# A hybrid decoder layer on one NeuronCore: the router's turned rows move to two one-tile buffers, two down weights are loaded earlier, and a mask moves by one unit

## The chip, the cores and the metric

The kernel runs on one core of one Trainium2 chip (trn2). The metric is the device time of one execution in microseconds (us). The profile is that of one execution, and times in it are us from the start of its span.

## The reference, cut to what matters

One layer (DEPTH is 1) on 512 tokens of width 1024, all in float32. Three residual blocks, then a final RMS norm:

```python
x = x + hybrid_mixer(rmsnorm(x, mix_norm_g), ...)       # 8 heads of forgetting attention | HGRN2 | convolution
x = x + cross_attention(rmsnorm(x, xatt_norm_g), mem_n, w_xq, w_xkv, w_xo)
x = x + hierarchical_moe(rmsnorm(x, ffn_norm_g), ...)   # 4 groups, top 1; 4 experts in a group, top 2
return rmsnorm(x, final_norm_g)
```

Forgetting attention adds to each score the difference of two cumulated log decays and masks it causally, then takes a softmax. In the mixture of experts a router picks one group and two of its four experts for each token; an expert is silu(h Wg) * (h Wu) times Wd, with Wg and Wu 1024 x 256 and Wd 256 x 1024, so 3 MB of weights for each of the 16 experts.

## The kernel before, in words

Each engine runs one list of instructions in order, and semaphores tie the lists together. The parts that the change touches are three.

**The attention over 16 units (lines 2104 to 2173 on TensorE, 1531 to 1597 on VectorE, 960 to 1006 on ScalarE).** A unit is one pair of heads and one block of 128 queries; four units make a pair of heads, and unit `u` has `u % 4 + 1` blocks of keys. In round `u` TensorE multiplies queries by keys (`qk(u)`, L2111), multiplies probabilities of unit `u - 3` by values (`pv`, L2133), turns the probabilities of unit `u - 2` (`pt`, L2120), and in some rounds does one product for the memory (L1904 or L1914) that fills the time. VectorE in round `u` adds the decay to the scores and takes the extremum (`f_scores(u)`, L1542), copies half of the turned probabilities (`f_pt(u - 2)`, L1560; ScalarE copies the other half, L973) and divides by the sums (`f_scale(u)`, L1553). The decays of a pair of heads come from `lf_dram` with four DMAs on the SP queue (`decay_sums`, L517). There are two buffers for them, so SP issues those of pair `p` (2 or 3) when the scores of pair `p - 2` are done. `f_mask(p)` (L1578, two instructions) adds the causal mask to the decays of pair `p`; it waits for their DMAs, and VectorE does it in round `4 (p - 1) + 1`, ahead of `f_pt`. The first scores of pair `p`, in round `4 p`, wait for it.

**The router.** After the cross attention TensorE multiplies by `w_xo` (L2180). In between, for each tile `t` of 128 tokens, it turns the rows of the residual (`turn_half`, L1674) into two PSUM banks. VectorE multiplies each bank by the norm's gain and writes it to `hT` (`turn_evac`, L1063, for stage 3), in the columns of tile `t`, so all four tiles have room of their own. TensorE multiplies `hT` by the router's weights (`logits_half`, L1680). The region `A[:, 7680:8704]` holds the final norm's gain (`fgain`), which SP loads at L535 behind two down weights; VectorE waits for it (`router_in`) before its last adds (L1333).

**The experts.** Rows of tokens are gathered into 12 passes (0 to 11) of 128 rows, and each pass serves two experts. TensorE does in pass `p`: gate and up (`gate_up_pass`, L1780, 64 matmuls), turning the next pass's rows (L1762), down of the pass before (`down_pass(p - 1)`, L1806, 32 matmuls), and turning the hidden rows (L1767). POOL gathers the rows of a pass (L648) and stores its result (L640). After the last passes it gathers each token's two results (L665), when the stores have landed.

The weights come on the SP queue in the order in which the passes take up experts (`TAKEN` is 0, 3, 1, 2, 4, 7, 5, 6, 8, 11, 9, 10, 12, 15, 13, 14). Gate and up have five homes (four slots of `W`, and `n_sb`); down weights have six, four in `Dn` and two in `hT` (`DN_HOME[e] >= SLOTS`, experts 4 and 7 first). SP's list (`experts_loads`, L519 to 584) is: down weights of 3 and 2; when the queries' projections are done (`freed(12)`, `freed(13)`), gate and up of 0 and 3; when cross attention is done (`xo_ps`), down weights of 0 and 1, and `fgain`; the normed rows to DRAM (L539); gate and up of 1, 2 and 4; then a wait for the last logits and for the rows of the second pass (`xg_in[1]`), and the down weights of 4 and 7 into `hT`; then, pass by pass, a wait for the pass that frees a home (`gu_ps`, `y_ps`) and the next loads (L476, L480, L488), 32 loads of 1 MB.

Expert weights first used in pass 9 are those of 12 and 15, in pass 10 those of 13, in pass 11 those of 14.

Of the kernel before, what the change touches and what calls it, by code (L numbers as in the profile page):

```python
# [10 lines left out]
ALU = mybir.AluOpType  # L11
# [3 lines left out]
P = 128  # L15
# [4 lines left out]
D = 1024  # L20
# [10 lines left out]
NG, NE = 4, 4  # L31
EX = NG * NE
# [3 lines left out]
DC = D // P  # L36
# [71 lines left out]
def build(nc, x, mem, mix_norm_g, w_in, fox_f_bias, fox_norm_g, hgrn_lb_logits, hgrn_norm_g,  # L108
# [3 lines left out]
    with ExitStack() as ctx:  # L112
# [87 lines left out]
        hidT = A[:, 5120:5632].rearrange("p (b k t) -> p b k t", b=2, k=2)  # L200
        ysb = A[:, 5632:7680].rearrange("p (b d) -> p b d", b=2)
        fgain = A[:, 7680:8704]

        room = [8704]

# [223 lines left out]
        def pair_end(u):  # L429

            return (u - PV_LAG) // ST if u >= PV_LAG and (u - PV_LAG) % ST == ST - 1 else None
# [50 lines left out]
        def load_gate_up(sp, e):  # L482
            load_gate(sp, e)
            load_up(sp, e)

        def load_down(sp, e):
            h = DN_HOME[e]
            sp.dma_start(dn_at[h], wd_e[e]).then_inc(dn_loaded[h], 16)  # L488
# [30 lines left out]
        def experts_loads(sp):  # L519

            sp.wait_ge(router_step, 6)
            sp.dma_start(y_dram[ZERO_ROW:ZERO_ROW + 1, :].rearrange("o (p n) -> (o p) n", p=P), zero8).then_inc(n_stored, 16)
            sp.wait_ge(x1_done, 8)
            for e in TAKEN[:DN_HOMES]:
                if DN_HOME[e] in (1, 3):
                    load_down(sp, e)
            for k in range(2):
                sp.wait_ge(*freed(12 + k))
                load_gate_up(sp, TAKEN[k])

            sp.wait_ge(xo_ps, 2 * XH)
            for e in TAKEN[:DN_HOMES]:
                if DN_HOME[e] in (0, 2):
                    load_down(sp, e)
            sp.dma_start(fgain, final_norm_g.rearrange("(o d) -> o d", o=1).to_broadcast([P, D])).then_inc(router_in, 16)  # L535

            def store_rows(t):
                sp.wait_ge(n_done, NORM0[3] + t + 1)
                sp.dma_start(n_dram[t * P:(t + 1) * P, :], nA[:, t, :]).then_inc(n_stored, 16)  # L539

            for t in range(ST - 1):
                store_rows(t)

            sp.wait_ge(*freed(14))
            load_gate(sp, TAKEN[2])
            store_rows(ST - 1)
            load_up(sp, TAKEN[2])
            load_gate_up(sp, TAKEN[3])
            load_gate_up(sp, TAKEN[4])
            sp.wait_ge(logits_ps, ST)  # L550
            sp.wait_ge(xg_in[1], 16)
            for e in TAKEN[:DN_HOMES]:
                if DN_HOME[e] >= SLOTS:
                    load_down(sp, e)

            for p in range(NP):
                if GU_REFILL[p]:
                    sp.wait_ge(gu_ps, p + 1)
                    for e in GU_REFILL[p]:
                        load_gate_up(sp, e)  # L560
                if p >= 1 and DN_REFILL[p - 1]:
                    sp.wait_ge(y_ps, 2 * p)
                    for e in DN_REFILL[p - 1]:
                        load_down(sp, e)

            sp.wait_ge(over_done, 1)
            with sp.If(sp.value_load(over[0:1, 0:1]) > 0):
                sp.wait_ge(y_ps, 2 * NP)
                with sp.Fori(0, OVER_PARTS * EX) as k:

                    e = k % EX
                    sp.dma_start(W[:, 0, :, 0:FF], wg_e[e]).then_inc(ov_w, 16)
                    sp.dma_start(W[:, 0, :, FF:2 * FF], wu_e[e]).then_inc(ov_w, 16)
                    sp.dma_start(Dn[:, 0], wd_e[e]).then_inc(ov_w, 16)
                    sp.wait_ge(ov_y_sb, 2 * k + 2)
                    sp.dma_start(ov_rows[k], ov_y).then_inc(ov_stored, 16)
            with sp.Else():
                pass
            for t in range(ST):
                sp.wait_ge(fin_out, t + 1)  # L580
                if t == ST - 1:
                    sp.wait_ge(fin_sq, ST + 1)
                sp.dma_start(out[0, t * P:(t + 1) * P, :], x_out[:, t, :]).then_inc(out_done, 16)
            sp.wait_ge(out_done, 16 * ST)
# [475 lines left out]
        def turn_evac(dve, stage, t, k, bank, dst, r0):  # L1060

            dve.wait_ge(turned, TURN0[stage] + 2 * t + k + 1)
            nc.vector.tensor_tensor(dst[:, 4 * k:4 * k + 4, t * P:(t + 1) * P], bank[:, :].rearrange("p (c t) -> p c t", c=4),  # L1063
                                    pc[:, r0 + 4 * k:r0 + 4 * k + 4].rearrange("p (c o) -> p c o", o=1).to_broadcast([P, 4, P]),
                                    ALU.mult).then_inc(turn_sb, 1)
# [5 lines left out]
        def experts_dve(dve):  # L1071
# [29 lines left out]
            def full_mean(t):  # L1101
                n = NORM0[3] + t
                dve.wait_ge(sq_done, NORM0[3] + 2 * t + 2)
                nc.vector.tensor_scalar(ss[:, n:n + 1], ss[:, n:n + 1], half_ss[:, t:t + 1], 1.0 / D, ALU.add, ALU.mult).then_inc(ms_done, 1)

            def choose(t):

                n = NORM0[3] + t
                dve.wait_ge(logits_ps, t + 1)
                dve.wait_ge(rstd_done, n + 1)  # L1110
                link(nc.vector.scalar_tensor_tensor(out=logits[:, t], in0=PS[6][:, t * (NG + EX):(t + 1) * (NG + EX)],
                                                    scalar=rstd[:, n:n + 1], in1=rbias, op0=ALU.mult, op1=ALU.add))
                sets = logits[:, t].rearrange("p (s k) -> p s k", k=4)
                steps[0] += 1
                nc.vector.tensor_tensor(above, across_rows(sets), across_cols(sets), ALU.is_ge).then_inc(route, 1)
                link(nc.vector.tensor_tensor(beats, across_rows(sets), across_cols(sets), ALU.is_gt))
                low = lower.rearrange("p (o i) j -> p o i j", o=1).to_broadcast([P, 1 + NG, 4, 4])
                link(nc.vector.copy_predicated(beats, low, above))
                link(nc.vector.tensor_reduce(rank, beats, AX_X, ALU.add))
                link(nc.vector.tensor_tensor(chosen[:, t], rank, limit, ALU.is_lt))  # L1120
                nc.vector.tensor_tensor(pickedb[:, t].rearrange("p (g e) -> p g e", g=NG), chosen[:, t, 1:],
                                        ghot[:, t].rearrange("p (g o) -> p g o", o=1).to_broadcast([P, NG, NE]), ALU.mult).then_inc(picked_done, 1)
                nc.vector.tensor_tensor(tokg16[:, t], ghot[:, t], tokid[:, t:t + 1].to_broadcast([P, NG]), ALU.mult).then_inc(pick_done, 1)
# [11 lines left out]
                    nc.vector.tensor_scalar(first_pick[:, t, r], pick[:, t, j, 0:r.stop - r.start], rstd[:, n:n + 1], ghot[:, t, 0:1],  # L1135
                                            ALU.mult, ALU.mult).then_inc(pick_done, 1)

            gains = pc[:, R_FFN:R_FFN + DC]

            def turned_rows(p):  # L1140

                if p >= 2:
# [10 lines left out]

            for t in range(ST):
                if t:
                    turn_evac(dve, 3, t - 1, 1, PS[5], hT, R_FFN)
                    full_mean(t - 1)
                    if t == 1:
                        dve.wait_ge(router_in, 16 * 4)
                        dve.wait_ge(router_const, 8)  # L1160
                    choose(t - 1)
                add_half(t, 0)
                turn_evac(dve, 3, t, 0, PS[4], hT, R_FFN)
                if t:
                    place(t - 1)
                first_mean(t)
                add_half(t, 1)
            turn_evac(dve, 3, ST - 1, 1, PS[5], hT, R_FFN)
            full_mean(ST - 1)
            choose(ST - 1)  # L1170
            place(ST - 1)
# [194 lines left out]
        def _(dve):  # L1366
# [215 lines left out]
            for u in range(UNITS + PV_LAG):  # L1582
                if u < UNITS:
                    for a in range(2):
                        f_scores(u, a)
                if pair_end(u) is not None:
                    f_out(pair_end(u))
                if u % ST == 1 and u < UNITS - ST:
                    f_mask(u // ST + 1)
                if TURN_LAG <= u < UNITS + TURN_LAG:  # L1590
                    f_pt(u - TURN_LAG)
                if u < UNITS:
                    for a in range(2):
                        f_scale(u, a)
                if u and pair_end(u - 1) is not None:
                    f_norm(pair_end(u - 1))
            f_norm(FH // 2 - 1)
# [68 lines left out]
        def experts_pe(pe, project_some):  # L1666
# [10 lines left out]
            def logits_half(t, k):  # L1677
                pe.wait_ge(turn_sb, TURN0[3] + 2 * t + k + 1)
                for c in range(4 * k, 4 * k + 4):
                    mm = nc.tensor.matmul(PS[6][:, t * (NG + EX):(t + 1) * (NG + EX)], hT[:, c, t * P:(t + 1) * P], wgr[:, c, :],  # L1680
                                          start=c == 0, stop=c == DC - 1)
                if k:
                    mm.then_inc(logits_ps, 1)
# [602 lines left out]
```

## Time and profile before

| what | value |
|---|---|
| median of 3 runs | 720.63 us (720.16 to 722.01) |
| the profiled execution's own time | 721.87 us |
| its span, first to last instruction | 720.1 us |
| PE busy | 683.2 us (95%) |
| DVE, ACT, POOL busy | 281.8, 152.1, 76.8 us |
| DMA | 111.91 MB, mean 155 GB/s |
| mean granted TensorE clock | 0.992 |
| chain that ended last | PE 80%, DMA 7%, SPq 4%, DVE 3%, ACT 3% |

The span has 1.8 us less than the execution's own time. PE is TensorE's matmuls, PEld its weight loads, DVE VectorE, ACT ScalarE, POOL GpSimd, SP the sync engine, SPq and POOLq their DMA issues. A line number is that of the helper which issues the instruction. "Idle before" is the time in which an engine did nothing ahead of an instruction, with what ended it; "issue" stands where no releaser was found in the records. The DMA share is the mean busy share of the core's 16 DMA engines, whose transfers overlap a little, so full use shows as somewhat over 1.

### The profile page before, as it was taken

How to read it: one execution, taken by the hardware profiler on the slowest of the kernel's cores; microseconds unless marked ns; L12 is line 12 of the kernel's file. 1: busy time of each engine (PE TensorE's matmuls, PEld its weight loads, DVE VectorE, ACT ScalarE, POOL GpSimd, SP SyncE). 2: the span in 40 equal slices, each digit the busy share in tenths (PEclk: the TensorE clock that was granted, in tenths of full speed). 3: DMA queues.
4: the chain of work that ended last, by engine and by line, in shares of the span. 5: the costliest groups of instructions: out<-in, count | busy, mean ns of one | idle time of the engine just before them, and what ended most of it. 6: DMA issues, size and time to landing. Idle time of an engine off the chain costs nothing.

```text
span 720.1 us, 8431 instructions
## 1 busy us (share of the span) xinstructions
PE 683.2 (95%) x3398; PEld 333.3 (46%) x3398; DVE 281.8 (39%) x673; ACT 152.1 (21%) x313; POOL 76.8 (11%) x106
## 2 busy tenths in 40 slices
PE   6999999999989899999999999999999999998993
PEld 4744444453547565444444446545564333332331
DVE  3207599927144564303120006413335712212156
ACT  3010351003282444211000003302111110101012
POOL 2000081502020000000000000000001110100052
PEclk9999999999999999999999999999999999999997
DMA  8903240303035513300019403030139999999773
GB/s 255 333 0 117 76 158 1 118 2 117 24 124 151 176 60 117 117 1 0 1 32 395 157 0 117 2 144 29 51 96 351 380 374 383 383 377 382 263 230 121
DMA packets 69941, 111.91 MB, mean 155 GB/s; under 512 B 5649, under 2 KB 43781, under 8 KB 69901
## 3 DMA queue, kind: packets, MB, share of 16 engines
q1 hardware_dynamic: 65724, 96.16, 38.8%
q0 software_dynamic: 4176, 15.21, 5.7%
q8 instruction: 27, 0.44, 0.3%
q14 instruction: 14, 0.11, 0.0%
HBM read 101.90 MB, written 9.46 MB: 155 GB/s over the span
## 4 chain that ended last, share of the span: by engine, by line
PE 80%; DMA 7%; SPq 4%; DVE 3%; ACT 3%; issue 1%; POOL 1%; DVEq 0%; POOLq 0%; ACTq 0%
PE bank L1904 26%; PE bank L2180 15%; PE bank L1780 8%; PE bank L1914 6%; PE bank L1806 3%; DMA W<-in_w_up_dram 2%; PE bank L2250 2%; PE bank L1950 2%; PE bank L2230 2%; DMA n_sb<-y_dram,A 2%; PE bank L1936 2%; PE bank L2133 1%; DMA x_sb<-in_x_dram 1%; SPq L480 1%; PE bank L2111 1%
## 5 line engine op out<-in xcount | busy, mean ns | idle before, releaser
L1904 PE MATMUL bank<-hT,W 128*128 128x512 f32 x368 | 159.7, 593 | 0.9 <-DVE hT L1063 0.9
L2180 PE MATMUL bank<-W,n_sb 128*128 128x512 f32 x256 | 114.2, 596 | 0.7 <-ACT n_sb L1031 0.7
L1904 PEld LDWEIGHTS bank<-hT,W 128*128 128x128 f32 x368 | 69.4, 190 | 87.5 <-issue 86.0
L1780 PE MATMUL bank<-W,A 128*32 128x512 f32 x672 | 84.8, 594 | 5.5 <-issue 2.4
L2180 PEld LDWEIGHTS bank<-W,n_sb 128*128 128x128 f32 x256 | 47.1, 190 | 53.9 <-issue 52.3
L1413 DVE SCALAR_TENSOR_TENSOR A<-A,pc 128x511 f32<-128x511 f32 (+29 forms) x60 | 51.6, 860 | 2.0
L1780 PEld LDWEIGHTS bank<-W,A 128*32 128x32 f32 x672 | 23.9, 110 | 52.9 <-issue 50.9
L695 POOL TENSOR_TENSOR rstd<-ss,mhalf 128x1 f32<-128x1 f32 x14 | 7.7, 549 | 372.8 <-DVE ss L1047 208.3
L1806 PE MATMUL bank<-Dn,A 128*32 128x512 f32 x264 | 36.3, 595 | 0.0
L1262 DVE TENSOR_TENSOR A<-A,bank 128x256 f32<-128x256 f32 x12 | 5.1, 421 | 75.8 <-ACT A L825 75.8
L898 ACT ACTIVATE A<-bank 128x512 f32<-128x512 f32 (+1 forms) x22 | 12.1, 556 | 103.7 <-PE bank L1904 77.0
L1904 PE MATMUL bank<-Dn,W 128*128 128x256 f32 x128 | 30.9, 397 | 1.2 <-DVE Dn L1063 1.0
L1621 DVE TENSOR_REDUCE fmx<-bank 128x1 f32<-128x256 f32 x16 | 6.7, 421 | 62.4 <-PE bank L2230 62.3
L1780 PE MATMUL bank<-n_sb,A 128*32 128x512 f32 x96 | 28.2, 594 | 0.0
L1914 PE MATMUL bank<-W,Dn 128*128 128x512 f32 x64 | 28.2, 594 | 0.0
L1904 PEld LDWEIGHTS bank<-Dn,W 128*128 128x128 f32 x128 | 24.9, 199 | 5.3 <-issue 1.2
L1806 PE MATMUL bank<-hT,A 128*32 128x512 f32 x120 | 25.4, 595 | 0.5 <-ACT A L832 0.5
L1478 DVE SCALAR_TENSOR_TENSOR states<-states,Dn,bank 128x64 f32<-128x64 f32 x64 | 17.9, 280 | 18.9 <-issue 13.9
L1063 DVE TENSOR_TENSOR hT<-bank,pc 128x512 f32<-128x512 f32 x24 | 16.0, 686 | 19.8 <-PE bank L1674 10.8
L825 ACT ACTIVATE A<-bank 128x256 f32<-128x256 f32 x12 | 4.6, 384 | 84.8 <-PE bank L1780 84.8
L964 ACT ACTIVATE hT<-hT,fmx 128x128 f32<-128x128 f32 (+3 forms) x32 | 17.7, 554 | 20.7 <-DVE fmx L1542 20.7
L1914 PE MATMUL bank<-W,hT 128*128 128x512 f32 x48 | 21.2, 594 | 0.0
(306 smaller groups left out, 806.8 us busy)
## 6 DMA issues: line engine op xcount, KB each, us to landing
W<-in_w_gate_dram SPq DMA_DIRECT2D x14, 1024.0 KB, 14.5
W<-in_w_up_dram SPq DMA_DIRECT2D x14, 1024.0 KB, 15.1
Dn<-in_w_down_dram SPq DMA_DIRECT2D x11, 1024.0 KB, 13.6
W<-in_w_in_dram SPq DMA_DIRECT2D x5, 2048.0 KB, 9.2
W<-in_w_xkv_dram SPq DMA_DIRECT2D x4, 2048.0 KB, 8.2
hT<-in_w_down_dram SPq DMA_DIRECT2D x5, 1024.0 KB, 12.9
y_dram<-A POOLq DMA_DIRECT2D x10, 512.0 KB, 7.0
W<-in_w_out_dram SPq DMA_DIRECT2D x2, 2048.0 KB, 7.8
```

The costliest lines, as they stand in the source:

```text
L964: nc.scalar.activation(fs[u % 3][a][:, 0:w], fs[u % 3][a][:, 0:w], ACT.Exp, bias=fmx[:, k:k + 1], scale=-1.0, accum_out=frs[:, k:k + 1]).t ...
L1063: nc.vector.tensor_tensor(dst[:, 4 * k:4 * k + 4, t * P:(t + 1) * P], bank[:, :].rearrange("p (c t) -> p c t", c=4), pc[:, r0 + 4 * k:r0 + ...
L1413: nc.vector.scalar_tensor_tensor(out=y[:, s:S], in0=a[:, 0:S - s], scalar=pc[:, r:r + 1], in1=y[:, s:S], op0=ALU.mult, op1=ALU.add).then_i ...
L1478: nc.vector.scalar_tensor_tensor(out=states[:, k + 1, :], in0=states[:, k, :], scalar=he4[:, p, k * CHUNK + CHUNK - 1:k * CHUNK + CHUNK], ...
L1780: mm = nc.tensor.matmul(PS[2 + b][r, :], xgT[:, b, c, r], gu_at[GU_HOME[e]][:, c, :], start=c == 0, stop=c == DC - 1)
L1806: mm = nc.tensor.matmul(PS[5 + n][r, :], hidT[:, p % 2, k, r], dn_at[DN_HOME[e]][:, k, 512 * n:512 * n + 512], start=k == 0, stop=k == 1)
L1904: mm = nc.tensor.matmul(bank[0:w, 0:n], lhs, src[:, c, 0:n], start=c == 0, stop=c == DC - 1)
L1914: mm = nc.tensor.matmul(bank[:, 0:w], src[:, c, t * P:(t + 1) * P], W[:, slot, c, col:col + w], start=c == 0, stop=c == DC - 1)
L1936: mm = nc.tensor.matmul(bank[:, 0:IW], hT[:, c, t * P:(t + 1) * P], w_if[:, c, :], start=c == 0, stop=c == DC - 1)
L1950: mm = nc.tensor.matmul(bank[:, :], lhs, hT[:, c, :], start=c == 0, stop=c == DC - 1)
L2180: mm = nc.tensor.matmul(PS[k % 4][:, :], src[:, c, t * P:(t + 1) * P], W[:, (n_load + n) % SLOTS, c, :], start=first and j == 0, stop=last ...
L2230: mm = nc.tensor.matmul(PS[u % 2][:, 0:M], xqT[:, 2 * h + k, t * P:(t + 1) * P], xkT[:, 2 * h + k, :], start=k == 0, stop=k == 1)
```

## The change

The router's turned rows go to `routeT`, two buffers of one tile, at `A[:, 4096:5120]` and `A[:, 7680:8704]`; tile `t` uses buffer `t % 2`, and `hT` isn't used by the router any more. The down weights of experts 4 and 7 are loaded right behind gate and up of expert 3, with no wait of their own, and the wait for the second pass's rows is gone. `fgain` shares its region with the second buffer, so its load moves behind all weights. `f_mask(p)` moves from round `4 (p - 1) + 1`, ahead of `f_pt`, to round `4 (p - 1) + 2`, behind `f_scale`.

```diff
--- before.py
+++ after.py
@@ -200,6 +200,7 @@
         hidT = A[:, 5120:5632].rearrange("p (b k t) -> p b k t", b=2, k=2)
         ysb = A[:, 5632:7680].rearrange("p (b d) -> p b d", b=2)
         fgain = A[:, 7680:8704]
+        routeT = [A[:, 4096:5120].rearrange("p (c t) -> p c t", c=DC), A[:, 7680:8704].rearrange("p (c t) -> p c t", c=DC)]
 
         room = [8704]
 
@@ -527,12 +528,14 @@
             for k in range(2):
                 sp.wait_ge(*freed(12 + k))
                 load_gate_up(sp, TAKEN[k])
+            for e in TAKEN[:DN_HOMES]:
+                if DN_HOME[e] >= SLOTS:
+                    load_down(sp, e)
 
             sp.wait_ge(xo_ps, 2 * XH)
             for e in TAKEN[:DN_HOMES]:
                 if DN_HOME[e] in (0, 2):
                     load_down(sp, e)
-            sp.dma_start(fgain, final_norm_g.rearrange("(o d) -> o d", o=1).to_broadcast([P, D])).then_inc(router_in, 16)
 
             def store_rows(t):
                 sp.wait_ge(n_done, NORM0[3] + t + 1)
@@ -547,11 +550,6 @@
             load_up(sp, TAKEN[2])
             load_gate_up(sp, TAKEN[3])
             load_gate_up(sp, TAKEN[4])
-            sp.wait_ge(logits_ps, ST)
-            sp.wait_ge(xg_in[1], 16)
-            for e in TAKEN[:DN_HOMES]:
-                if DN_HOME[e] >= SLOTS:
-                    load_down(sp, e)
 
             for p in range(NP):
                 if GU_REFILL[p]:
@@ -563,6 +561,8 @@
                     for e in DN_REFILL[p - 1]:
                         load_down(sp, e)
 
+            sp.wait_ge(logits_ps, ST)
+            sp.dma_start(fgain, final_norm_g.rearrange("(o d) -> o d", o=1).to_broadcast([P, D])).then_inc(router_in, 16)
             sp.wait_ge(over_done, 1)
             with sp.If(sp.value_load(over[0:1, 0:1]) > 0):
                 sp.wait_ge(y_ps, 2 * NP)
@@ -1103,6 +1103,15 @@
                 dve.wait_ge(sq_done, NORM0[3] + 2 * t + 2)
                 nc.vector.tensor_scalar(ss[:, n:n + 1], ss[:, n:n + 1], half_ss[:, t:t + 1], 1.0 / D, ALU.add, ALU.mult).then_inc(ms_done, 1)
 
+            gains = pc[:, R_FFN:R_FFN + DC]
+
+            def route_evac(t, k):
+
+                dve.wait_ge(turned, TURN0[3] + 2 * t + k + 1)
+                nc.vector.tensor_tensor(routeT[t % 2][:, 4 * k:4 * k + 4, :], PS[4 + k][:, :].rearrange("p (c t) -> p c t", c=4),
+                                        gains[:, 4 * k:4 * k + 4].rearrange("p (c o) -> p c o", o=1).to_broadcast([P, 4, P]),
+                                        ALU.mult).then_inc(turn_sb, 1)
+
             def choose(t):
 
                 n = NORM0[3] + t
@@ -1135,8 +1144,6 @@
                     nc.vector.tensor_scalar(first_pick[:, t, r], pick[:, t, j, 0:r.stop - r.start], rstd[:, n:n + 1], ghot[:, t, 0:1],
                                             ALU.mult, ALU.mult).then_inc(pick_done, 1)
 
-            gains = pc[:, R_FFN:R_FFN + DC]
-
             def turned_rows(p):
 
                 if p >= 2:
@@ -1153,19 +1160,19 @@
 
             for t in range(ST):
                 if t:
-                    turn_evac(dve, 3, t - 1, 1, PS[5], hT, R_FFN)
+                    route_evac(t - 1, 1)
                     full_mean(t - 1)
                     if t == 1:
                         dve.wait_ge(router_in, 16 * 4)
                         dve.wait_ge(router_const, 8)
                     choose(t - 1)
                 add_half(t, 0)
-                turn_evac(dve, 3, t, 0, PS[4], hT, R_FFN)
+                route_evac(t, 0)
                 if t:
                     place(t - 1)
                 first_mean(t)
                 add_half(t, 1)
-            turn_evac(dve, 3, ST - 1, 1, PS[5], hT, R_FFN)
+            route_evac(ST - 1, 1)
             full_mean(ST - 1)
             choose(ST - 1)
             place(ST - 1)
@@ -1585,13 +1592,13 @@
                         f_scores(u, a)
                 if pair_end(u) is not None:
                     f_out(pair_end(u))
-                if u % ST == 1 and u < UNITS - ST:
-                    f_mask(u // ST + 1)
                 if TURN_LAG <= u < UNITS + TURN_LAG:
                     f_pt(u - TURN_LAG)
                 if u < UNITS:
                     for a in range(2):
                         f_scale(u, a)
+                if u % ST == 2 and u < UNITS - ST:
+                    f_mask(u // ST + 1)
                 if u and pair_end(u - 1) is not None:
                     f_norm(pair_end(u - 1))
             f_norm(FH // 2 - 1)
@@ -1677,7 +1684,7 @@
             def logits_half(t, k):
                 pe.wait_ge(turn_sb, TURN0[3] + 2 * t + k + 1)
                 for c in range(4 * k, 4 * k + 4):
-                    mm = nc.tensor.matmul(PS[6][:, t * (NG + EX):(t + 1) * (NG + EX)], hT[:, c, t * P:(t + 1) * P], wgr[:, c, :],
+                    mm = nc.tensor.matmul(PS[6][:, t * (NG + EX):(t + 1) * (NG + EX)], routeT[t % 2][:, c, :], wgr[:, c, :],
                                           start=c == 0, stop=c == DC - 1)
                 if k:
                     mm.then_inc(logits_ps, 1)
```

## Rows read from the trace of the kernel before

**Rows 1.** Busy by stage: us; PE, PEld, DVE, ACT, POOL; PEclk; DMA share, GB/s.
```profile
440.00:466.00 26.00, 25.06 (x98) 15.78 (x96) 15.44 (x52) 10.33 (x29) 0.00 (x0) 1.00 0.00 1
...
544.00:653.00 109.00, 105.35 (x930) 35.65 (x930) 37.34 (x111) 13.42 (x29) 13.95 (x18) 1.00 1.07 377
```

**Rows 2.** PE, order of time, passes 2, 9, 10: start, us, what [idle before].
```profile
565.67 7.07 PE L1780 MATMUL bank<-W,A 128*32 128x512 f32 x64
...
653.24 7.07 PE L1780 MATMUL bank<-W,A 128*32 128x512 f32 x64 [1.53 <-DMA W<-in_w_up_dram]
...
667.71 7.07 PE L1780 MATMUL bank<-W,A 128*32 128x512 f32 x64 [2.44 <-issue]
```

**Rows 3.** SP, order of time: start, us the issue took, what.
```profile
551.06 4.12 SPq L488 DMA_DIRECT2D hT<-in_w_down_dram  x2
...
555.23 1.19 SPq L476 DMA_DIRECT2D W<-in_w_gate_dram  x1
...
574.91 0.62 SPq L476 DMA_DIRECT2D W<-in_w_gate_dram  x1
...
637.13 6.05 SPq L480 DMA_DIRECT2D W<-in_w_up_dram  x1
...
648.76 8.03 SPq L480 DMA_DIRECT2D W<-in_w_up_dram  x1
...
666.94 3.88 SPq L488 DMA_DIRECT2D hT<-in_w_down_dram  x1
```

**Rows 4.** DMA issues, us to landing last: those of 555.23, 637.13, 648.76, 666.94.
```profile
W<-in_w_gate_dram SPq DMA_DIRECT2D x1, 1024.0 KB, 15.6
...
W<-in_w_up_dram SPq DMA_DIRECT2D x1, 1024.0 KB, 16.0
...
W<-in_w_up_dram SPq DMA_DIRECT2D x1, 1024.0 KB, 18.9
...
hT<-in_w_down_dram SPq DMA_DIRECT2D x1, 1024.0 KB, 12.7
```

**Rows 5.** Chain that ended last, 238 to 249: start, us, what.
```profile
238.66 7.92 DMA A<-lf_dram
...
247.89 0.61 DVE hT L1560
```

**Rows 6.** PE, order of time, the stall in round 6.
```profile
248.63 1.10 PE L2133 MATMUL bank<-hT,A 128*64 128x128 f32 x16 [1.95 <-DVE hT L1560]
```

**Rows 7.** VectorE, order of time: a mask, and the scores of rounds 3, 7, 11.
```profile
229.34 1.29 DVE L1578 TENSOR_TENSOR Dn<-Dn,causal 128x256 f32<-128x256 f32 x2 [2.05 <-DMA Dn<-lf_dram]
...
235.89 0.69 DVE L1542 CUSTOM_DVE_ANT_0 hT<-bank,A 128x512 f32<-128x512 f32 x1 [1.87 <-PE bank L2111]
...
254.66 0.69 DVE L1542 CUSTOM_DVE_ANT_0 hT<-bank,Dn 128x512 f32<-128x512 f32 x1 [2.45 <-PE bank L2111]
...
271.63 0.69 DVE L1542 CUSTOM_DVE_ANT_0 hT<-bank,A 128x512 f32<-128x512 f32 x1 [2.44 <-PE bank L2111]
```

**Rows 8.** Groups of 466 to 680: a dense and a spread target.
```profile
L1147 DVE TENSOR_TENSOR A<-bank,pc 128x512 f32<-128x512 f32 x24 | 15.5, 682 | 1.1 <-PE bank L1719 1.0
...
L1063 DVE TENSOR_TENSOR hT<-bank,pc 128x512 f32<-128x512 f32 x8 | 5.5, 692 | 10.8 <-PE bank L1674 10.8
```

**Rows 9.** The page, part 5: weight loads from two layouts.
```profile
L1904 PEld LDWEIGHTS bank<-hT,W 128*128 128x128 f32 x368 | 69.4, 190 | 87.5 <-issue 86.0
...
L1904 PEld LDWEIGHTS bank<-Dn,W 128*128 128x128 f32 x128 | 24.9, 199 | 5.3 <-issue 1.2
```

**Rows 10.** DMA issues, us to landing last: those of 466.97 and 467.44.
```profile
Dn<-in_w_down_dram SPq DMA_DIRECT2D x1, 1024.0 KB, 7.0
...
A<-in_final_norm_g_dram SPq DMA_DIRECT2D x1, 512.0 KB, 7.8
```

**Rows 11.** Chain that ended last, where the passes end.
```profile
680.69 3.21 DMA y_dram<-A
```

**Rows 12.** The page, part 6: POOL's stores.
```profile
y_dram<-A POOLq DMA_DIRECT2D x10, 512.0 KB, 7.0
```


## The prediction

> **What bounds the kernel now.** I read the table of busy time by stage first: it shows which resource is full in which stretch. In the twelve expert passes up to 653 PE is busy 105.4 of 109 us, and the DMA engines are full too, at 1.07 and 377 GB/s [rows 1]. Of two full resources the one that ends a wait is the bound, so PE's order of time is next: two passes start late, pass 9 by 1.53 us, for an up weight, and pass 10 by 2.44 us, where no releaser was found [rows 2]. The issues with their landings name that one. Expert 15's up weight, issued at 637.13, landed 16.0 later at 653.1, just ahead of pass 9's start at 653.24; expert 13's, issued at 648.76, landed 18.9 later at 667.7, and pass 10 starts at 667.71 [rows 2 to 4]. So TensorE sets the pace of the passes, but the weights run so close behind that TensorE loses 1.53 + 2.44 = 3.97 us to them.
>
> Did weights come late because SP issued them late, or because the engines were full? In SP's order of time the issues themselves last several us (8.03, 6.05, 4.12) and follow each other: SP pushes into a full queue [rows 3]. Expert 7's gate (issued 555.23) landed at 570.8, expert 14's down at 679.6, with 31 loads of 1 MiB between: 3.51 us each [rows 3, 4].
>
> The third reading is the chain of waits through the attention. It runs over the decays' transfer (issued 238.66, 7.92 us), the mask and VectorE's copy `f_pt(3)`, which stands behind the mask and was done at 248.5 [rows 5]; PE then stood 1.95 us [rows 6]. Its 1.95 us are the only stall that the mask's place makes.
>
> **Part 1: two down weights earlier.** Removed from the full stretch are two loads (experts 4 and 7, 2.10 MB) and the wait ahead of them. How far does everything behind them come forward? With POOL's traffic unchanged the engines need 2 x 3.51 = 7.0 us less. The lower bound is bytes alone, 2.10 MB at 377 GB/s, 5.6 us [rows 1]. I take 7.0, since POOL's gathers and stores are tied to the passes and don't grow, and keep 5.6 as the other end. Needed for no stall: expert 15's up weight 1.5 us earlier, and expert 13's 3.97 earlier, since pass 10 then starts 1.53 + 2.44 earlier. Even 5.6 covers that, with 1.6 us to spare. So 3.97 come off, from 0 to 3.97 in the range.
>
> Next in line is the release of homes. SP can't issue expert 5's gate before pass 1's gate and up end, or expert 6's before pass 2's, at 565.67 + 7.07 = 572.7; before, it did so at 574.91, only 2.2 us later [rows 2, 3]. After the change SP does wait there. It costs nothing if the engines still have work: a load lands some 15 us after its issue [rows 4], and with 7.0 taken off about 7 us of transfers are still queued at 572.7. From there on SP again pushes into a full queue.
>
> The two loads go out right behind gate and up of expert 3, near 433, and move past nothing that is pressed for time: SP's next wait ends with the cross attention at 466, and from 440 to 466 the engines carry 1 GB/s [rows 1]. Their 2.10 MB take 5.6 us of these 26. Cost 0; without this cover they would cost what they cost now. Their target `hT` is free, as the queries' last product is what SP waits for there. The wait for the second pass's rows (`xg_in[1]`) goes as well: the issues at 551.06 [rows 3] stood behind it, and its time is within the 7.0.
>
> **Part 2: the router's buffers.** VectorE has the same eight evacuations, now with a dense target. The nearest rows are 692 ns for the spread target `hT` and 682 for a dense one [rows 8]: -0.08 us for eight, nothing. TensorE's 64 weight loads read another layout; by the rows of two layouts (190 and 199 ns [rows 9]) that is 64 x 9 ns = 0.6 us either way at most, and they run beside matmuls. I take 0 and keep -0.6 to +0.6. No wait is added: VectorE writes a buffer a second time only after TensorE has turned the tile two later, which on its list stands behind the products that read the buffer.
>
> **Part 3: the final gain.** Its load leaves 467 and goes to the end of SP's list. At 467.44 it landed 7.8 us after its issue, at 475.2, and the down weight before it (466.97 + 7.0) at 474.0, so its own part is 1.2 us; these are the bounds [rows 10]. The wait for the last logits that is put before it is long met. Expert 14's down lands at 679.6 - 7.0 = 672.6, and with 1.2 the gain is there at 673.8. Whom can it delay? POOL's last store, which ends the chain of the passes (issued 680.69, landed 3.21 later [rows 11]) and would be issued at 680.69 - 3.97 = 676.7, 2.9 us behind it. Cost 0, up to 3.7 if it took all of its 7.8 from 672.6 (to 680.4). VectorE needs it only in its last adds, after the gathers that follow this store.
>
> **Part 4: the mask one unit later.** The same six instructions, 1.29 us a pair [rows 7]. In round 1 the mask waited 2.05 us for its transfer, but PE lost nothing. In round 5 the copy no longer stands behind it: it can follow `pt(3)` at once, and `pv(3)` follows TensorE's `qk(6)`: 1.95 us come off. In its new place the mask stands between `f_scale` of round 2, 6 or 10 and the scores of the next round, before which VectorE is idle 1.87, 2.45 and 2.44 us [rows 7]. The mask of 1.29 fits in each. Its transfer is there at 246.6 (238.66 + 7.92 [rows 5]). Round 6 reaches the mask at about 250: VectorE was free 2.45 us ahead of 254.66, at 252.2, and all that is 1.95 earlier. If one didn't fit, it would cost up to 1.29, three of them 3.9. I take 0.
>
> **Sum.** 3.97 + 1.95 = 5.92 us. The profiled execution took 721.87, so its like would take 715.95; it stood 1.24 above the median of 720.63, so I forecast 714.7. The two savings add, because all behind 250 shifts together: the loads' waits there are for TensorE's own progress.
>
> **The rivals.**
> *A, both savings* (the forecast): 714.7. For it: 1.6 us to spare at pass 10 even by the lower bound, and 1.87 - 1.29 = 0.6 at the tightest mask.
> *B, the mask finds a new victim.* The scores of round 7 come late, or ScalarE's half of the copy becomes what `pv` waits for, and the 1.95 stay. Against it: 2.45 idle us for 1.29. 720.63 - 3.97 = 716.7.
> *C, the queue follows its releases.* If the loads come forward only by as much as expert 6's gate can be issued earlier (2.2 us) and not by the bytes saved, expert 13's up weight lands at 665.5, and of 3.97 only 2.2 come off: 720.63 - 1.95 - 2.2 = 716.5. Against it: about 7 us of transfers are queued at that time.
> *D, hidden anyway.* TensorE's late starts have another cause than the weights, and it merely moves on from the attention's stall to another: 719 to 720.6. Pass 10's missing releaser speaks for it, the landings to 0.1 us against it.
> *E, slower: the gain at the tail.* SP's list keeps its pace, the last weight still lands at 679.6, and behind it come the gain's 0.5 MB. At the upper bound it lands at 687.4, and if POOL's last store, issued at 680.7, has to stand behind it, all gathers start 6.7 us later: 720.63 - 1.95 + 6.7 = 725.4. It decides from a landing after 680.7 + 1.95 + 2.2 = 684.9. Against it: its own part was 1.2 us, and POOL's stores landed 7.0 us after issue, in the middle [rows 12], beside weights that took 13 to 19 [rows 4].
> The Trainium skill's "DMA: Bandwidth & Descriptors" (section "Queues, rings and completion order") bears on E: each DMA engine goes round the queues that have work for it, so a store of POOL's shares with SP's queue and doesn't stand behind it. By that rule, the trace agrees, as its stores landed twice as fast as SP's loads, and E shrinks to the time of the gain's own 0.5 MB. The same page (section "Anatomy of one DMA") gives an estimate for a lone transfer of 2.0 us and the bytes at 436 GB/s, 3.2 us for the gain, where the trace has 1.2 behind another; by 3.2 it lands at 675.8, still ahead of the store.
>
> **How the numbers follow.** What a measurement can tell from no change is 0.3%, 2.2 us, so faster means under 718.5. A 0.60, B 0.12, C 0.16: all faster, 0.88. D 0.08: the same. E 0.04: slower. The range has to hold 8 in 10: A, with 0.6 for the router's loads and the runs' own spread below (714.7 - 1.3 = 713.4), and B and C above, with the same 0.6, to 717.3. D and E are left out.
>
> **What would show it.** In the changed profile: passes 9 and 10 start 12.0 us after the one before, with no idle time for a weight; the up weights of 15 and 13 land 5 us and more ahead of them; the last down weight lands about 7 us earlier against pass 11, and the gain before POOL's last store. SP shows a real wait before expert 6's gate. The round-6 stall of 1.95 is gone, VectorE's masks stand in its idle time, and no scores of rounds 3, 7 and 11 start behind one. The passes' DMA share stays at 1.07 but ends earlier. It is wrong if PE's idle time before pass 9 or 10 stays (C or D), if `pv` in round 6 still waits (B), or if the last store takes much over 3.2 us (E).

## The result, and the profile after

In five runs of each, the changed kernel took a median of 713.46 us (712.26 to 714.91) against 720.63 (717.93 to 722.01) before: a ratio of 0.9896, 95% interval 0.9872 to 0.992. Faster by 7.5 us by the ratio (9.2 to 5.8 by its interval), where 5.9 were forecast; 0.9896 x 720.63 = 713.1 lies 0.3 below the low end of the range.

| profiled execution | before | after |
|---|---|---|
| time, span, us | 721.87, 720.1 | 714.91, 713.2 |
| PE on the chain that ended last | 80% | 87% |
| DMA and SPq on that chain | 7% and 4% | 4% and 0% |
| mean granted clock | 0.992 | 0.991 |

Line numbers behind 1150 are 7 higher in the changed kernel (L1780 is L1787, L1904 is L1911), SP's loads 1 higher. Three lines of the page after: the span, the engines' busy time, and the chain by engine.

```profile
span 713.2 us, 8430 instructions
...
PE 682.8 (96%) x3398; PEld 332.3 (47%) x3398; DVE 282.0 (40%) x673; ACT 152.0 (21%) x313; POOL 76.0 (11%) x106
...
PE 87%; DMA 4%; DVE 3%; ACT 3%; issue 1%; POOL 1%; SPq 0%; DVEq 0%; POOLq 0%; ACTq 0%
```

PE holds 87% of the chain, and SP's queue is off it. The next view is busy time by stage, beside [rows 1] (columns as there).

```profile
440.00:466.00 26.00, 24.37 (x91) 14.69 (x90) 12.87 (x44) 9.86 (x27) 0.00 (x0) 1.00 0.10 34
544.00:650.00 106.00, 104.11 (x926) 35.37 (x922) 34.99 (x99) 12.11 (x27) 12.67 (x17) 1.00 1.07 377
```

The two down weights, issued from 430.05 on, are mostly in by 440 and all near 442: only their last 0.7 MB fall between 440 and 466, where there was nothing (34 GB/s for 1). The passes run at the same 1.07 and 377 GB/s. PE in order of time (start, us, what, idle before and its releaser) tells what that brought:

```profile
215.43 5.38 PE L1911 MATMUL bank<-Dn,W 128*128 128x256 f32 x16 [0.99 <-DVE Dn L1063]
...
246.04 1.09 PE L2140 MATMUL bank<-hT,A 128*64 128x128 f32 x16
...
247.34 3.62 PE L1911 MATMUL bank<-Dn,W 128*128 128x256 f32 x16
...
563.00 7.07 PE L1787 MATMUL bank<-W,A 128*32 128x512 f32 x64
...
588.57 0.63 PE L1823 MATMUL bank<-identf,states 128*128 128x128 f32 x4 [1.14 <-DVE A L1262]
...
648.96 7.07 PE L1787 MATMUL bank<-W,A 128*32 128x512 f32 x64
...
660.92 7.07 PE L1787 MATMUL bank<-W,A 128*32 128x512 f32 x64
```

Passes 9 and 10 start 12.0 us after the pass before, with no idle time: the 1.53 and 2.44 of [rows 2] are gone. So is the 1.95 of [rows 6]: the products at 246.04 follow without a gap. Left in the passes are 0.78 and 0.76 ahead of the first two, and the 1.14 at 588.57. The row at 215.43 is for later: 16 products that take 5.38 us here and 3.62 to 3.72 elsewhere in the attention. The kernel before has the like of it:

```profile
216.11 5.38 PE L1904 MATMUL bank<-Dn,W 128*128 128x256 f32 x16 [0.98 <-DVE Dn L1063]
```

This also dates the difference. The two traces are 0.68 us apart here, by chance in the first loads; after the mask's stall 2.7, behind passes 9 and 10 6.8, and at the end 6.9. So the profiled pair gained 0.7 (chance) + 2.0 + 4.1 + 0.1.

SP's order of time (start, us the issue took), then four of its landings (us from issue to landing, last: those of 626.64, 638.65, 656.48 and 662.54), then the store of the chain's end:

```profile
430.05 2.60 SPq L489 DMA_DIRECT2D hT<-in_w_down_dram  x2
...
562.76 2.64 SPq L489 DMA_DIRECT2D Dn<-in_w_down_dram  x1
...
570.13 0.37 SPq L477 DMA_DIRECT2D W<-in_w_gate_dram  x1
...
626.64 6.57 SPq L481 DMA_DIRECT2D W<-in_w_up_dram  x1
...
638.65 7.42 SPq L481 DMA_DIRECT2D W<-in_w_up_dram  x1
...
656.48 6.02 SPq L489 DMA_DIRECT2D hT<-in_w_down_dram  x1
...
662.54 0.71 SPq L565 DMA_DIRECT2D A<-in_final_norm_g_dram  x1
```

```profile
W<-in_w_up_dram SPq DMA_DIRECT2D x1, 1024.0 KB, 18.1
...
W<-in_w_up_dram SPq DMA_DIRECT2D x1, 1024.0 KB, 21.0
...
hT<-in_w_down_dram SPq DMA_DIRECT2D x1, 1024.0 KB, 15.3
...
A<-in_final_norm_g_dram SPq DMA_DIRECT2D x1, 512.0 KB, 10.4
```

```profile
673.91 3.20 DMA y_dram<-A
```

The early pair is issued at 430.05. SP comes to expert 6's gate at 565.4 and then really waits, until pass 2's gate and up end at 563.00 + 7.07 = 570.07. Expert 15's up weight lands at 644.7, 4.2 us ahead of pass 9, expert 13's at 659.6, 1.3 ahead of pass 10. Expert 14's down lands at 671.8, the gain at 672.9, and POOL's last store, issued at 673.91, takes 3.20, as before [rows 11]. Last, VectorE's masks in their new place:

```profile
232.79 1.29 DVE L1585 TENSOR_TENSOR Dn<-Dn,causal 128x256 f32<-128x256 f32 x2
...
235.21 0.69 DVE L1549 CUSTOM_DVE_ANT_0 hT<-bank,A 128x512 f32<-128x512 f32 x1 [1.12 <-PE bank L2118]
...
249.53 1.28 DVE L1585 TENSOR_TENSOR A<-A,causal 128x256 f32<-128x256 f32 x2
...
252.06 0.69 DVE L1549 CUSTOM_DVE_ANT_0 hT<-bank,Dn 128x512 f32<-128x512 f32 x1 [1.25 <-PE bank L2118]
...
268.96 0.69 DVE L1549 CUSTOM_DVE_ANT_0 hT<-bank,A 128x512 f32<-128x512 f32 x1 [1.24 <-PE bank L2118]
```

Each mask follows other work at once, and the scores behind it still wait for PE (1.12, 1.25 and, in round 11, 1.24 us): it fits.

### The profile page after: what moved, and what is told of

Read it like the earlier page. It is cut to its first block, busy times and chain, and to the rows that moved or that the text cites. A ratio compares the mean times of both kernels' runs of the same rounds, so it can differ in the third digit from the quotient of the medians.

```text
span 713.2 us, 8430 instructions
## 1 busy us (share of the span) xinstructions
PE 682.8 (96%) x3398; PEld 332.3 (47%) x3398; DVE 282.0 (40%) x673; ACT 152.0 (21%) x313; POOL 76.0 (11%) x106
## 4 chain that ended last, share of the span: by engine, by line
PE 87%; DMA 4%; DVE 3%; ACT 3%; issue 1%; POOL 1%; SPq 0%; DVEq 0%; POOLq 0%; ACTq 0%
PE bank L1911 26%; PE bank L2187 16%; PE bank L1787 11%; PE bank L1921 6%; PE bank L1813 5%; PE bank L2257 2%; PE bank L1957 2%; PE bank L2237 2%; PE bank L2140 2%; DMA n_sb<-y_dram,A 2%; PE bank L1943 2%; PE bank L1769 1%; PE bank L2118 1%; DMA x_sb<-in_x_dram 1%; PE bank L2127 1%; PE bank L2029 1%
## 5 line engine op out<-in xcount | busy, mean ns | idle before, releaser
L1911 PE MATMUL bank<-hT,W 128*128 128x512 f32 x368 | 159.7, 593 | 0.9 <-DVE hT L1063 0.9
L1911 PEld LDWEIGHTS bank<-hT,W 128*128 128x128 f32 x368 | 69.4, 190 | 87.5 <-issue 86.0
L1787 PE MATMUL bank<-W,A 128*32 128x512 f32 x672 | 84.8, 594 | 1.5 <-DVE A L1154 1.5
L1787 PEld LDWEIGHTS bank<-W,A 128*32 128x32 f32 x672 | 23.2, 110 | 49.5 <-issue 47.6
L1911 PE MATMUL bank<-Dn,W 128*128 128x256 f32 x128 | 30.9, 397 | 1.2 <-DVE Dn L1063 1.0
L1787 PE MATMUL bank<-n_sb,A 128*32 128x512 f32 x96 | 28.2, 594 | 0.0
L1911 PEld LDWEIGHTS bank<-Dn,W 128*128 128x128 f32 x128 | 24.9, 199 | 5.3 <-issue 1.2
L1095 DVE TENSOR_TENSOR x_sb<-x_sb,bank 128x512 f32<-128x512 f32 x8 | 5.5, 688 | 33.6 <-PE bank L2187 33.6
```

Of the source, the lines that this page charges most:

```text
L1787: mm = nc.tensor.matmul(PS[2 + b][r, :], xgT[:, b, c, r], gu_at[GU_HOME[e]][:, c, :], start=c == 0, stop=c == DC - 1)
L1911: mm = nc.tensor.matmul(bank[0:w, 0:n], lhs, src[:, c, 0:n], start=c == 0, stop=c == DC - 1)
```

## The experiments

Theory: the two savings add, and nothing else happens. Where runs came out above its sum, the rival was that each wait had a price beyond its length. All ratios are to the kernel before, run in the same session; its medians were 722.00, 722.13 and 721.71.

### Each part alone

**The mask alone:** the kernel before with the diff's last hunk but one, `f_mask` at `u % ST == 2` behind `f_scale`.

> The kernel before with the mask alone moved. Theory (two independent savings): the 1.95 us stall in round 6 is gone, the passes keep about 4.0 us of late starts, and the time is 2.0 us under before (ratio 0.997). Rival (the attention's saving is larger than read, because a later stall goes with it): 3 us or more under before, with PE's idle sum between 220 and 310 lower by more than 2.1.

**The loads alone:** the change, with `f_mask` left in its old place.

> The change without the mask's move. Theory: round 6 keeps its 1.95 us, passes 9 and 10 have no stall, 4.0 to 4.2 us under before (ratio 0.994). Rival (the last part of the surprise, 7.2 for 5.9, comes from the loads, in runs whose stalls in the passes are larger than the profiled one's): 5 us or more under before.

**The buffers alone:** `routeT`, `route_evac` and the gain at the end of SP's list; down weights and mask as before.

> The two router buffers and the gain's load at the end; the two down weights back in their old place with both waits, the mask in its old place. Theory: nothing moves, within 0.6 us of before, and passes 9 and 10 start late by 4.0 us together. Rival (the buffers themselves give the missing us, by their dense layout): 1 us under before, with shorter rows in the router.

**The change once more.**

> The changed kernel once more. Theory: the surprise is the runs' spread: 5.9 to 6.3 us under before of the same session (ratio 0.9915), and PE's first stretch up to 30 us varies by some 0.7 us from profile to profile. Rival (a real further saving): 7 us again (ratio 0.990).

| kernel | median us | ratio (95%) |
|---|---|---|
| mask alone | 718.95 | 0.9969 (0.9953 to 0.9985) |
| loads alone | 715.06 | 0.9917 (0.9896 to 0.9939) |
| buffers alone | 721.95 | 1.0004 (0.9987 to 1.002) |
| change again | 713.57 | 0.9889 (0.9865 to 0.9913) |

By the ratios the mask gives 2.2 us (forecast 1.95), the buffers nothing, the loads 6.0 where 3.97 were forecast: most of the excess sits with the loads. PE's order of time in the mask's kernel, then in the buffers' (lines 9 higher than before), shows where:

```profile
664.69 8.77 PE L1780 MATMUL bank<-W,A 128*32 128x512 f32 x64 [2.66 <-issue]
```

```profile
651.40 7.07 PE L1789 MATMUL bank<-W,A 128*32 128x512 f32 x64 [0.83 <-DMA W<-in_w_up_dram]
...
666.16 8.62 PE L1789 MATMUL bank<-W,A 128*32 128x512 f32 x64 [2.72 <-issue]
```

Pass 10's 64 products took 8.77 and 8.62 us in these profiles, 7.07 in [rows 2]. The buffers' kernel by stretches (columns of [rows 1]) says why:

```profile
640.00:651.00 11.00, 10.57 (x98) 3.42 (x86) 2.31 (x4) 1.36 (x3) 1.10 (x2) 1.00 1.06 381
664.00:667.00 3.00, 0.84 (x5) 0.24 (x9) 0.00 (x0) 0.00 (x0) 0.56 (x1) 0.82 1.04 381
667.00:675.00 8.00, 8.00 (x67) 2.42 (x60) 0.00 (x0) 0.15 (x1) 0.00 (x0) 0.85 1.08 380
675.00:680.00 5.00, 5.00 (x46) 1.87 (x48) 2.17 (x4) 1.04 (x3) 0.00 (x0) 1.00 0.43 167
```

The granted clock fell about when the wait ended and came back inside the pass: at the lower of its two levels (1.2 of 2.4 GHz), 0.82 of 3 us and 0.85 of 8 us make 1.1 + 2.4 = 3.5 us, and half of that is lost where PE has work. DMA stays at 381 and 380 GB/s, so the weights aren't what slows the products. The Trainium skill has this in "TensorE: Matmul & The Clock Gate" (section "HAM oscillation — how this bites in real kernels"): a wait for DMA between groups of matmuls lets the array be throttled again, and the next group starts at the lower clock. The trace agrees, with 8.62 - 7.07 = 1.55 us behind a wait of 2.72, though the waits in the page's own example are longer, 3 to 5 us. The profile of before that the prediction rests on happened to keep its clock there.

The router's own rows, in the buffers' kernel:

```profile
L1113 DVE TENSOR_TENSOR A<-bank,pc 128x512 f32<-128x512 f32 x8 | 5.5, 692 | 10.8 <-PE bank L1683 10.8
```

692 ns for the evacuation, as in [rows 8].

### Is it the wait that costs the clock?

**Filled:** the kernel before, with four products that nothing reads in pass 10, ahead of the wait for its weights.

```diff
                 pe.wait_ge(xt_sb, 2 * p + 2)
+                if p == 10:
+                    keep_busy(4, PS[0])
```

> The kernel before, with four more matmuls of scanmask by identf into bank 0 (their product is not used) ahead of pass 10, in the time in which TensorE waits for expert 13's weights; nothing is loaded earlier. Theory (the wait before pass 10 costs its own 2.4 to 2.7 us and, in part of the executions, 1.6 more, since the granted clock then falls to half for a stretch): no half clock around pass 10, the matmuls of the pass in 7.07 and not 8.6 to 8.8 us, and 0.5 to 1.2 us under before (ratio 0.9985), though TensorE does 2 us more work. Rival (the fall is not tied to the wait): the same time as before or up to 0.5 us more, and half clock in pass 10 in some profiles.

**Three more profiles of it, and three of the kernel before.**

> The kernel before with pass 10's wait filled. Theory (the wait brings the fall of the clock): pass 10's 64 matmuls take 7.07 us in this look and in the next two. Rival (the fall goes with the late weights): 8.4 to 8.8 us in most of the three.

> As in the look before it: 7.07 us for pass 10's gate and up if the wait is the cause, 8.4 to 8.8 if not.

> As in the look before it: 7.07 us for pass 10's gate and up if the wait is the cause, 8.4 to 8.8 if not.

> The kernel before, looked at once more, for how often the granted clock falls at pass 10. Theory: passes 9 and 10 wait 3.5 to 4.5 us together in each look, and in more than half of the looks pass 10's gate and up take 8.6 to 8.8 us at half clock for a part. Rival (e1 and e3 were chance): 7.07 in all looks.

> As the look before it: more than half of these looks with half clock in pass 10, or none.

> As the look before it: more than half of these looks with half clock in pass 10, or none.

Filled took 721.91, ratio 0.9988 (0.997 to 1.0006): no change that can be told, 0.9 us by the means. So the times don't decide here, the profiles do. The filler (each product leaves two records) costs 0.7: from pass 9 to pass 10 it is 15.40 us in its four profiles, 14.70 on the mean of six with the bare wait. PE in its second profile, then in the first further profile of the kernel before:

```profile
663.74 3.60 PE L1664 MATMUL bank<-scanmask,identf 128*128 128x512 f32 x8
...
667.27 7.07 PE L1780 MATMUL bank<-W,A 128*32 128x512 f32 x64
```

```profile
246.67 1.09 PE L2133 MATMUL bank<-hT,A 128*64 128x128 f32 x16 [2.35 <-DVE hT L1560]
...
248.17 5.08 PE L1904 MATMUL bank<-Dn,W 128*128 128x256 f32 x16
...
667.25 8.77 PE L1780 MATMUL bank<-W,A 128*32 128x512 f32 x64 [2.87 <-issue]
```

The pass behind the filler took 7.07 in four profiles of four. Behind the bare wait it took 8.77, 8.43 and 8.77 in the three further profiles (waits of 2.87, 2.58 and 2.73). With the two above and the first profile, the clock fell in 5 of 6 profiles with that wait, in none of 4 with it filled. The same data, the same weights, the same place: the idle time is the cause. The further profiles show it a second time: at 248.17, behind the mask's stall, the 16 products took 5.08 for 3.62. By stretches:

```profile
243.00:246.00 3.00, 1.32 (x9) 0.54 (x7) 1.37 (x3) 0.73 (x3) 0.00 (x0) 1.00 0.03 9
246.00:249.00 3.00, 2.33 (x20) 2.04 (x21) 2.93 (x11) 1.05 (x3) 0.00 (x0) 0.79 0.00 0
249.00:252.00 3.00, 3.00 (x10) 2.45 (x9) 1.18 (x5) 0.94 (x4) 0.00 (x0) 0.65 0.00 0
252.00:255.00 3.00, 3.00 (x18) 1.65 (x17) 0.64 (x3) 0.39 (x1) 0.00 (x0) 1.00 0.00 0
```

Ten profiles have the mask's stall (before, loads alone, buffers alone, the three further ones of before, filled's four), and in five of them the clock fell behind it: the three further ones, and two of filled. Of the six without stall or filler (the change three times, mask alone, and one early and late turn below) none has a fall there. The other fall of the attention, near 215, comes ahead of the stall and stands in 3 of those ten and 2 of these six: it has nothing to do with the change. No profile has both: the five falls behind the stall are all among the seven of those ten that had none near 215.

### Do the loads follow the bytes?

**One early:** the change, with only expert 4's down early; expert 7's goes behind gate and up of expert 4 (`TAKEN[4]`; the expectation calls it expert 2), with no wait.

```diff
             for e in TAKEN[:DN_HOMES]:
-                if DN_HOME[e] >= SLOTS:
+                if DN_HOME[e] == SLOTS:
                     load_down(sp, e)
...
             load_gate_up(sp, TAKEN[4])
+            for e in TAKEN[:DN_HOMES]:
+                if DN_HOME[e] == SLOTS + 1:
+                    load_down(sp, e)
```

> The change, but only expert 4's down weight is loaded early; expert 7's goes out behind gate and up of expert 2, with no wait. Theory (bytes): one load is worth 2.7 us, half of the 5.4 that two brought, so pass 9 starts with no wait, pass 10 waits 4.0 - 2.7 = 1.3 us, the clock mostly holds, and the time is 1.3 us above the changed kernel. Rival (the queue follows its releases, so the removed wait was what mattered): no wait at either pass, and the changed kernel's time.

714.68, ratio 0.9898 (0.9873 to 0.9923). PE in this kernel (lines 10 higher than before):

```profile
660.25 7.07 PE L1790 MATMUL bank<-W,A 128*32 128x512 f32 x64 [1.30 <-issue]
```

Pass 9 doesn't wait, pass 10 waits 1.30: the margin of 1.3 that the change had there has become a wait of 1.3, so one load is worth 2.6 us, against 1.05 MB at 377 GB/s = 2.8 and a spacing of 3.51. If the queue followed its releases, taking one load back in would have changed nothing. And after 1.30 the pass still takes 7.07: this wait did not cost the clock. The 1.3 us above the changed kernel that were expected don't show in the times: 0.9898 beside the change's 0.9889 and 0.9896 is 0.1 to 0.7 us, and the intervals cover each other.

### What was left

**Late turn:** the change, with the late tiles turned in passes 2 and 4 instead of 2 and 3 (`if p in (2, 4): turn_late(p // 2 - 1)` on TensorE's list, `if p in (3, 5): late_turned((p - 3) // 2)` on VectorE's).

> The change, with the second turning of the late rows behind pass 4 instead of pass 3. Theory: the 1.14 us in which TensorE waits for VectorE's copy ahead of pass 4 are gone, nothing takes their place as the weights have 1.4 us to spare at pass 10: but then pass 10 starts 1.1 us earlier too, and 0.3 us are left; 1.1 us under the changed kernel, 0.8 if the weights bind again.

**Kept busy:** the change, with two unread products ahead of each of two waits of the attention's start.

```diff
             g = run([along(1, 3, 0, FW)], g, 5)
+            keep_busy(2, PS[2])
...
             pe.wait_ge(ho_rs, HP)
+            keep_busy(2, PS[2])
             pe.wait_ge(turn_sb, TURN0[2])
```

> The change, with two more matmuls into bank 2 (product not used) at each of TensorE's two idle times near 213 and 215. Theory: the half clock that follows there in part of the executions (5.38 for 3.69 us in the 16 matmuls behind it) is gone, the two kinds of runs become one, and the median falls by 0.5 to 1.5 us. Rival (the fall has another cause): half clock stays in the profile, or the time is as the changed kernel's.

**Both:**

> The change with both of the last two edits, the later turning of the late rows and the matmuls that keep TensorE busy near 213 and 215. Theory (they add up): 1.1 us and, in the median, about 0.8 us more under before than the changed kernel, so a ratio of 0.986 to 0.987, and in the profile no half clock before the last gathers and no wait at pass 10. Rival (with both, the weights bind at pass 10 again): a wait of up to 1 us there, ratio 0.988.

| kernel | median us | ratio (95%) |
|---|---|---|
| late turn | 713.06 | 0.9875 (0.9848 to 0.9901) |
| kept busy | 713.12 | 0.9878 (0.9853 to 0.9903) |
| both | 711.91 | 0.9872 (0.9842 to 0.9902) |

Late turn loses the 1.14 of 588.57. In its profile pass 10 starts 12.18 us behind pass 9 (657.52 and 645.34) where it was 11.96, so some 0.2 of it come back there; in that of both it is 11.97. Kept busy, at the two waits:

```profile
214.50 1.88 PE L1671 MATMUL bank<-scanmask,identf 128*128 128x512 f32 x4
...
216.21 3.62 PE L1911 MATMUL bank<-Dn,W 128*128 128x256 f32 x16
```

3.62 for the 16 products that took 5.38 and 5.17 in two of the six profiles with neither stall nor filler, 3.69 in the others. The fillers cost 0.6 us: from the products at 204.94 to those at 215.43 it was 10.49 in the change, here, from 205.04 to 216.21, 11.17, and one gap behind is 0.07 shorter. Both together is the fastest median of all, but its interval and those of the two alone cover each other. A last profile of the change had 712.39 us, no wait at passes 9 and 10, and 3.69 at its row of 215:

> The changed kernel once more: pass 9 and 10 without a wait and at full clock; near 216 the clock may fall or not (it did in one of two profiles), never near 248, where the mask's wait is gone.

### The ledger

Each timed run comes with its mean granted clock. (1 - clock) x time is what the lower level would cost if TensorE had work all the while; before it was 6.3 to 7.1 us a run, in the means of three sessions. Not all of that is lost. In all 18 profiles the clock goes to the lower level behind TensorE's last product and stays there to the end. The change again, by stretches:

```profile
705.00:712.40 7.40, 0.00 (x0) 0.00 (x0) 2.19 (x4) 0.72 (x1) 1.36 (x2) 0.61 0.54 214
```

PE is idle there, so these 0.39 x 7.4 = 2.9 us cost nothing, and they are all that this run's clock of 0.996 stands for. By profile this end makes 2.8 to 4.6 us; in the four profiles of before its mean is 3.8, in the three of the change 3.6, so it nearly cancels in a difference. Each kernel's gain can then be put together from the waits that its edit takes away, by the profile, and the clock's share, by the runs, and set against the difference of the mean times:

| kernel | runs | waits | clock | sum | measured |
|---|---|---|---|---|---|
| mask alone | 12 | 1.95 | 0.3 | 2.2 | 2.5 |
| loads alone | 6 | 3.97 | 2.1 | 6.0 | 6.3 |
| buffers alone | 12 | 0 | -0.2 | -0.2 | -0.4 |
| change again | 6 | 5.92 | 2.2 | 8.1 | 8.0 |
| filled | 12 | -0.7 | 1.5 | 0.8 | 0.9 |
| one early | 6 | 4.62 | 3.3 | 8.0 | 7.7 |
| late turn | 6 | 7.06 - 0.2 | 2.5 | 9.4 | 9.5 |
| kept busy | 6 | 5.92 - 0.6 | 3.7 | 9.0 | 9.0 |
| both | 6 | 7.06 - 0.6 | 2.9 | 9.3 | 9.1 |

The kernels before ran 23, 17 and 11 times beside them. All rows close to 0.3 us (the minus terms are what fillers cost, and for late turn the 0.2 at pass 10). The clock comes from the same runs as the times, so the check lies in what is left without it: measured less clock is 2.2 for the mask, 4.3 for the loads and 5.8 for the change, against waits of 1.95, 3.97 and 5.92, and no other cause of that size is needed. The clock's column itself is uncertain by 0.9 to 1.4 us a row (two standard errors of the difference). So the mask's 0.3 can't be told from the 0.8 that the profiles make of it, nor the loads' 2.1 from their 1.3; that the wait ahead of pass 10 is the dearer of the two is what the profiles say (1.3 and 0.8), not shown by the runs.

## Why the prediction was off by two microseconds

**The bound, the places, the sign: right.** TensorE lost 3.97 us to late weights and 1.95 to the mask, and both went in full (rows of 648.96, 660.92 and 246.04).

**The step that failed: the Sum.** "3.97 + 1.95 = 5.92 us" prices each wait at its own length. What stood in its place is 5.92 + 2.2 for the clock = 8.1, measured 8.0 (the change again, by the means); 7.5 by the ratio of the first comparison, whose interval holds both 5.92 and 8.1. The clock's term, by rows: 1.4 to 1.7 behind the wait ahead of pass 10 (8.43 to 8.77 for 7.07), in 5 profiles of 6, is 1.3 on the mean; behind the mask's stall, 1.4 to 1.7 in 5 of 10, 0.8 (5.08 to 5.30 for 3.62 in four of them; in one 4.45, and 1.68 for 1.09 in the group ahead). The trace of before held one row of this kind, at 216.11, 16 products at 5.38 beside others at 3.7; the prediction read waits only, and its range had no term for the clock. One such fall (5.38 - 3.69 = 1.7) would have put its low end at 713.4 - 1.7 = 711.7.

**Part 1.** The loads came forward by bytes. Taking off the 2.67 us by which everything behind the attention was earlier, expert 15's up landed (653.1 - 644.7) - 2.67 = 5.7 us earlier, expert 13's 5.3, expert 14's down 5.2. So the end of 5.6 was right and not the 7.0 that was taken: 3.51 us a load counted POOL's traffic as if it shrank with the loads. It cost nothing since 5.6 covered the 3.97, as the text said, though the margin at pass 10 was 1.3 and not 3. SP's real wait before expert 6's gate came as told and delayed nothing.

**Part 2.** 0, by the buffers' kernel: 1.0004, and 692 ns for the same evacuation.

**Part 3.** 0. The gain landed 1.2 us behind the last down weight (forecast 1.2), 1.0 ahead of the last store (forecast 2.9, short by the term of part 1). The 3.2 us that the prediction estimated for a lone transfer don't show behind another; the Trainium skill's "DMA: Bandwidth & Descriptors" (section "Anatomy of one DMA") gives that fit for transfers that GpSimd issues, and the gain is issued by SP. Rival E falls with 3.20 us for that store.

**Part 4.** The stall went, by 2.0 in the profiled pair and 2.2 by the ratio of the mask alone (1.1 to 3.4 by its interval), and no new victim came: rival B falls with the rows of 235.21 and 252.06.

**Rivals C and D.** C falls with one early: its 1.30 us at pass 10 are those of the bytes. D falls with the gaps of passes 9 and 10 closing as their weights came earlier.

## What to carry to other kernels

Before you price a wait on TensorE at its own length, compare the duration of the like group of products behind it with others: if it is longer at the same shape, the clock fell, and the wait's removal is worth that too. One profile can't tell this, as the clock falls in some executions and not in others; several profiles can, and the mean granted clock of many runs, beside that of the kernel before, as a part of it is the idle end. When loads leave a full stretch, count their bytes at the measured rate, not the mean spacing of one queue's loads.

## What was unexpected of the hardware

A single wait of 2.6 to 2.9 us, in a stretch where PE is otherwise busy for 97% of the time [rows 1], came with a fall of the granted clock in 5 of 5 profiles, and 2.44 in the profile of before did not; 1.30 did not either. Four unread products in its place held the clock in 4 of 4, and cost 0.7 us of the 1.4 to 1.7 that they save. Two at each of two waits in the attention came with clocks of 0.994 to 0.996 in all six runs of kept busy and 0.993 to 0.996 in those of both, where the change had 0.991 to 0.996. What decides whether the clock falls behind the mask's stall, as waits of 1.9 to 2.4 us go both ways, stays open.
